# A decoder block: q and k projected with tokens on partitions, turned there, then transposed

## The reference

```
def partial_rotary(t, cos, sin):
    half = ROT_DIM // 2                       # 8
    t1 = t[..., :half]; t2 = t[..., half:ROT_DIM]
    r1 = t1 * cos - t2 * sin
    r2 = t2 * cos + t1 * sin
    return concatenate([r1, r2, t[..., ROT_DIM:]], axis=-1)

h = modulate(rms_norm(x, g_mix), sh1, sc1)
u, q, k, v, ga, gb = split(h @ w_in)
y_ssm = s5_mixer(u, ...)                      # complex diagonal recurrence over the 256 tokens
qh, kh = partial_rotary(heads(q)), partial_rotary(heads(k))
o = causal_attention(qh, kh, heads(v))        # one block of 256 keys
merged = sigmoid(ga) * glu(gelu(y_ssm)) + sigmoid(gb) * (o @ w_attn_o)
x = x + gt1 * (merged @ w_out)
x = x + gt2 * top4_of_32_experts(modulate(rms_norm(x, g_ffn), sh2, sc2))
out = rms_norm(x, g_final)
```

## Time and profile before

| | us |
|---|---|
| median of 3 runs | 1171.04 (1170.08 to 1172.61) |
| profiled execution, whole | 1169.95 |
| its span, first to last instruction | 1168.1 |
| TensorE busy in the span | 1125.0 (96%) |
| VectorE / ScalarE / GpSimd busy | 452.4 / 138.2 / 107.8 |
| DMA, mean over the span | 393 GB/s |

### The profile page before, as it was taken

One profiled execution on the slowest core, in us unless ns is written; L12 is line 12 of the kernel. 1 busy time (PEld: TensorE's weight loads), 2 busy tenths in 40 slices (PEclk: granted clock), 3 DMA queues, 4 the chain that ended last, 5 costly groups with the idle time before them and its releaser, 6 DMA issues.

```text
span 1168.1 us, 17323 instructions
## 1 busy us (share of the span) xinstructions
PE 1125.0 (96%) x7015; PEld 502.1 (43%) x7015; DVE 452.4 (39%) x960; ACT 138.2 (12%) x299; POOL 107.8 (9%) x142
## 2 busy tenths in 40 slices
PE   6999999999999999999999999999999999999996
PEld 5867788654333333333333333333333333333332
DVE  5897767462233222333332223222222222222234
ACT  3213231141000000000000000000000000000002
POOL 2878730000000000000000000000000000000000
PEclk9999999999999999999999999999999999999998
DMA  9993379979999999999999999999999999999995
GB/s 346 320 383 114 108 271 388 418 285 427 422 429 429 430 430 430 431 431 431 435 431 431 431 431 431 430 430 431 430 431 431 431 431 430 431 431 424 429 424 212
DMA packets 49090, 459.53 MB, mean 393 GB/s; under 512 B 8944, under 2 KB 9396, under 8 KB 26784
## 3 DMA queue, kind: packets, MB, share of 16 engines
q1 hardware_dynamic: 48176, 458.19, 94.0%
q10 hardware_dynamic: 880, 0.86, 0.2%
HBM read 457.99 MB, written 1.05 MB: 393 GB/s over the span
## 4 chain that ended last, share of the span: by engine, by line
PE 76%; DMA 19%; DVE 2%; ACT 1%; issue 1%; SPq 1%; DVEq 0%
PE ps L1039 28%; DMA ring<-in_w_gu 16%; PE ps L1081 16%; PE ps L610 8%; PE ps L1014 4%; PE ps L958 3%; PE ps L807 2%; DMA ring<-in_w_down 2%; PE ps L1061 2%; PE ps L825 2%; PE ps L790 1%; PE ps L882 1%; PE ps L607 1%; DMA ring<-in_w_ada 1%; PE ps L1069 1%
## 5 line engine op out<-in xcount | busy, mean ns | idle before, releaser
L1081 PE MATMUL ps<-ring,tmp 128*64 128x512 f32 x1024 | 227.0, 595 | 11.2 <-ACT tmp L1299 9.7
L1039 PE MATMUL ps<-ring,zone 128*64 128x512 f32 x1024 | 227.2, 596 | 10.8 <-DMA ring<-in_w_gu 10.8
L1039 PE MATMUL ps<-zone 128*64 128x512 f32 x1024 | 227.0, 596 | 0.2 <-DVE zone L1731 0.2
L1798 DVE TENSOR_TENSOR x_tok<-x_tok,ps 128x512 f32<-128x512 f32 x128 | 82.0, 682 | 261.1 <-PE ps L1014 258.7
L1081 PEld LDWEIGHTS ps<-ring,tmp 128*64 128x64 f32 x1024 | 83.5, 137 | 134.0 <-issue 130.8
L1039 PEld LDWEIGHTS ps<-ring,zone 128*64 128x64 f32 x1024 | 70.6, 137 | 163.1 <-issue 142.6
L1039 PEld LDWEIGHTS ps<-zone 128*64 128x64 f32 x1024 | 70.6, 137 | 152.8 <-issue 146.2
L1296 ACT ACTIVATE hT<-hT 128x256 f32<-128x256 f32 x64 | 23.9, 417 | 725.0 <-DVE hT L1813 725.0
L610 PE MATMUL ps<-hT,ring 128*128 128x256 f32 x448 | 101.5, 382 | 0.9 <-DVE hT L1463 0.9
L1813 DVE TENSOR_SCALAR hT<-ps 128x256 f32<-128x256 f32 x64 | 24.2, 420 | 191.4 <-PE ps L1039 191.4
L610 PEld LDWEIGHTS ps<-hT,ring 128*128 128x128 f32 x448 | 83.6, 190 | 14.4 <-issue 3.5
(11 more groups left out here) (330 smaller groups left out, 828.1 us busy)
## 6 DMA issues: line engine op xcount, KB each, us to landing
ring<-in_w_down SPq DMA_DIRECT2D x61, 2048.0 KB, 18.6
zone<-in_w_gu SPq DMA_DIRECT2D x23, 4096.0 KB, 27.7
ring<-in_w_gu SPq DMA_DIRECT2D x23, 4096.0 KB, 31.3
zone<-in_w_gu SPq DMA_DIRECT2D x14, 2048.0 KB, 12.9
ring<-in_w_gu SPq DMA_DIRECT2D x13, 2048.0 KB, 13.8
ring<-in_w_ada SPq DMA_DIRECT2D x24, 1024.0 KB, 13.0
ring<-in_w_in SPq DMA_DIRECT2D x16, 1024.0 KB, 14.2
ring<-in_w_gu SPq DMA_DIRECT2D x10, 1024.0 KB, 9.1
```

The costliest lines, as they stand in the source:

```text
L1039: last = mm(ps[CAP * h:CAP * h + CAP, b, :], hg[:, 2 * j + kk, :], w[:, kk, D * b + 512 * h:D * b + 512 * h + 512], start=False, stop=(j = ...
L1081: last = mm(ps[CAP * h:CAP * h + CAP, 3, :], actT[:, q, j, :], w[:, q, 512 * h:512 * h + 512], start=False, stop=(j == DN_PIECES - 1 and q ...
L1798: V.tensor_tensor(x_tok[:, t, 512 * h:512 * h + 512], x_tok[:, t, 512 * h:512 * h + 512], ps[:, bank + h, :], ALU.add).then_inc(S["comb_ad ...
```

## The change

q and k are projected in v's form, tokens on partitions, into `q_tok` and `k_tok`, which are other views of the buffers `qT` and `kT`. VectorE turns the first 16 dimensions of each head there with four instructions per tensor, in place. TensorE then transposes the tile in eight 128x128 pieces into two PSUM banks, and ScalarE copies these back over the same buffer, now with channels on partitions. The cosine and sine tables shrink to 32 columns each and the permutation goes, so the constants in HBM have 600 columns in place of 1432. `rotary(0)` moves into the middle of VectorE's last doubling, ahead of the nop for which GpSimd waits; `rotary(1)` stays between the first two recurrences. The second tensor's TensorE part (`turned_columns(1)`) comes after two of the four blocks of `proj(3, 0)`, where the permutation came after one.

```
--- before.py
+++ after.py
@@ -49,8 +49,9 @@
 
 
 C_ID, C_TRI, C_SLOT, C_TRI32, C_ID32, C_Q, C_E, C_MB, C_MC, C_SL = 0, 128, 256, 320, 352, 384, 400, 401, 403, 405
-C_COS, C_SIN, C_ROT, C_CAUSAL = 408, 664, 920, 1048
-C_ALL = 1432
+C_COS, C_SIN, C_CAUSAL = 408, 440, 472
+C_ALL = 600
+C_BIAS = 408
 BF16 = mybir.dt.bfloat16
 
 R_C, R_GMIX, R_D, R_ADA, R_WIDE, R_GFFN, R_ALL = 0, 8, 16, 20, 36, 68, 76
@@ -66,19 +67,12 @@
     p = np.arange(P)
     c[:, C_ID:C_ID + P] = np.eye(P)
     inv = (1.0 / THETA ** (np.arange(0, 2 * HALF, 2, dtype=np.float32) / (2 * HALF))).astype(np.float32)
-    ang = np.arange(T, dtype=np.float32)[None, :] * inv[p % HALF][:, None]
-    turned = (p % HD < 2 * HALF)[:, None]
-    c[:, C_COS:C_COS + T] = np.where(turned, np.cos(ang), 1.0)
-    c[:, C_SIN:C_SIN + T] = np.where(turned, np.sin(ang), 0.0)
-    for j in range(P):
-        if j % HD < HALF:
-            c[j + HALF, C_ROT + j] = -1.0
-        elif j % HD < 2 * HALF:
-            c[j - HALF, C_ROT + j] = 1.0
+    ang = (np.arange(TT, dtype=np.float32)[None, :, None] * P + p.astype(np.float32)[:, None, None]) * inv[np.arange(2 * HALF) % HALF]
+    c[:, C_COS:C_COS + 2 * HALF * TT] = np.cos(ang).reshape(P, -1)
+    c[:, C_SIN:C_SIN + 2 * HALF * TT] = (np.sin(ang) * np.repeat([-1.0, 1.0], HALF)).reshape(P, -1)
     c[:, C_TRI:C_TRI + P] = p[:, None] < p[None, :]
     past = np.where(p[None, :] <= p[:, None], 0.0, -1e30)
     c[:, C_CAUSAL:C_CAUSAL + P] = past
-    c[:, C_CAUSAL + 2 * P:C_CAUSAL + 3 * P] = past
     c[:, C_SLOT:C_SLOT + CAP] = np.arange(1, CAP + 1)
     e = np.arange(EXPERTS)
     c[:EXPERTS, C_TRI32:C_TRI32 + EXPERTS] = e[:, None] <= e[None, :]
@@ -107,7 +101,7 @@
     x_tok = sb("x_tok", [P, TT, D])
     xn_tok = sb("xn_tok", [P, TT, D])
     hT = sb("hT", [P, KD, T])
-    cst = sb("cst", [P, C_ALL])
+    cst = sb("cst", [P, C_BIAS + D])
     ones = sb("ones", [P, P])
     cols = sb("cols", [P, R_ALL])
     mod = sb("mod", [P, 6 * KD])
@@ -131,6 +125,7 @@
     esin = cut(ST * T).rearrange("p (s t) -> p s t", s=ST)
     qT = cut(KW * T).rearrange("p (m t) -> p m t", m=KW)
     kT = cut(KW * T).rearrange("p (m t) -> p m t", m=KW)
+    q_tok, k_tok = (a.rearrange("p m t -> p (m t)").rearrange("p (i n) -> p i n", i=TT) for a in (qT, kT))
     oT = cut(KW * T).rearrange("p (m t) -> p m t", m=KW)
     v_tok = cut(TT * W).rearrange("p (i n) -> p i n", i=TT)
     BT = cut(2 * KW * P).rearrange("p (r m n) -> p r m n", r=2, m=KW)
@@ -217,7 +212,7 @@
     wr2 = ptmp[:, 256:512].rearrange("p (k e) -> p k e", k=KD)
     gfin_row = [xn_tok[32 * h:32 * h + 1, 0, 0:W] for h in range(2)]
     poswt, pickwT = xn_tok[:, 1, 0:2 * T], xn_tok[:, 1, 2 * T:3 * T]
-    brow = cst[:, C_COS:C_COS + D]
+    brow = cst[:, C_BIAS:C_BIAS + D]
     rowT = brow[3 * EXPERTS:P, 0:2 * T].rearrange("p (j t) -> p j t", j=2)
     wr = probs[:, 0:256].rearrange("p (k e) -> p k e", k=KD)
     rt = probs[:, 256:640].rearrange("p (j i e) -> p j i e", j=6, i=TT)
@@ -245,7 +240,7 @@
     more_rows_in, more_cols_up, shift_set = sem("more_rows_in"), sem("more_cols_up"), sem("shift_set")
     names = """x_in const_in rows_in ssm_in late_in gfin_in out_stored ones_set cols_up cols_sb cond_set ssm_rows sprm_up sprm_sb Bblk_set Cblk0_set
         Cblk1_set BT_up CT0_up CT1_up BT_sb CT0_sb CT1_sb phases modrow_sb modT_up mod1_sb sq1 xn1 xT_up
-        hD_sb hA_sb proj_sb bu_up scanned xs_set xs_read rot_up rot_read rope_set sc_up negmax expd probs
+        hD_sb hA_sb proj_sb bu_up scanned xs_set xs_read rotated turned_up turned_sb sc_up negmax expd probs
         probsT_up probsT_sb o_up o_sb mod2_sb row_up row_sb y_skip gelu sig_ga sig_gb sigb_set ya_set
         yb_used merged out_up x1 sq2 xn2 x2T_up h2_sb logit_up top_set ex_set sel_set pos_up pos_sb pos_half rT_up
         rT_sb extra_set cum_up hot_set item_up item_sb hotb_set pick_set hg_up hg_sb gated sig_set
@@ -337,7 +332,7 @@
         return wo[:, 2 * n:2 * n + 2, :]
 
     PROJ_BANK = (0, 2, 0, 2, 0, 0, 0, 4)
-    ROT_BANK = (2, 0)
+    TURN_BANK = (2, 0)
     MOD_BANK = {1: 6, 2: 2}
     LAST_BANK = (6, 0)
     GU_PIECES, DN_PIECES = 4, 2
@@ -421,7 +416,7 @@
 
             for n in range(place["in", 3] + 1):
                 load_piece(n)
-            sp.dma_start(cst[:, P:], const[:, P:]).then_inc(S["const_in"], 16)
+            sp.dma_start(cst[:, P:C_ALL], const[:, P:]).then_inc(S["const_in"], 16)
             for r, (b, cc) in enumerate(((b_re, c_re), (b_im, c_im))):
                 sp.dma_start(b_in[:, r], b[0].rearrange("(s q) p c -> (q p) s c", q=2)).then_inc(S["const_in"], 16)
                 sp.dma_start(c_in[:, r], cc[0].rearrange("(m g) c p -> (g c) m p", m=KW)).then_inc(S["const_in"], 16)
@@ -591,9 +586,9 @@
                     elif g < 4:
                         pe.wait_ge(S["proj_sb"], g - 1)
                         if g == 3:
-                            pe.wait_ge(S["rot_read"], 1)
+                            pe.wait_ge(S["turned_sb"], 1)
                     elif g == 4:
-                        pe.wait_ge(S["rot_read"], 2)
+                        pe.wait_ge(S["turned_sb"], 2)
                     elif g < 7:
                         pe.wait_ge(S["proj_sb"], g)
                     else:
@@ -602,8 +597,8 @@
                     k = 4 * h + kk
                     if g == 0:
                         pe.wait_ge(S["hA_sb" if k % 4 > 1 else "hD_sb"], 2 * h + k % 2 + 1)
-                    if g == 3:
-                        for i in range(TT):
+                    if 1 <= g <= 3:
+                        for i in range(ms[0] // 2, ms[-1] // 2 + 1):
                             last = mm(ps[:, b + i, :], hT[:, k, P * i:P * i + P], w[:, kk, :], start=(k == 0), stop=(k == KD - 1))
                     else:
                         for m in ms:
@@ -662,22 +657,22 @@
                                                Cblk[:, r, m].rearrange("p q n -> p (q n)"), ident)
                 last.then_inc(S[f"CT{r}_up"], 1)
 
-            def rotate(src, n):
+            def turned_columns(n):
 
                 pe.wait_ge(S["proj_sb"], 2 + n)
-                pe.wait_ge(S["const_in"], 80)
+                pe.wait_ge(S["rotated"], n + 1)
                 for m in range(KW):
-                    last = mm(ps[:, ROT_BANK[n] + m // 2, (m % 2) * T:(m % 2) * T + T], cst[:, C_ROT:C_ROT + P], src[:, m, :],
-                              start=True, stop=True, skip_group_check=True)
-                last.then_inc(S["rot_up"], 1)
-
+                    for i in range(TT):
+                        c0 = (m % 2) * T + P * i
+                        last = nc.tensor.transpose(ps[:, TURN_BANK[n] + m // 2, c0:c0 + P], (q_tok, k_tok)[n][:, i, P * m:P * m + P], ident)
+                last.then_inc(S["turned_up"], 1)
 
             HEAD_BANK = (2, 3)
 
             def scores(p):
 
                 if p == 0:
-                    pe.wait_ge(S["rope_set"], 2)
+                    pe.wait_ge(S["turned_sb"], 2)
                     pe.wait_ge(S["proj_sb"], 4)
                     pe.wait_ge(S["mask_set"], 2)
                 else:
@@ -725,15 +720,15 @@
             proj(1, 1)
             proj(2, 0)
             b_columns()
-            rotate(qT, 0)
+            turned_columns(0)
             c_columns(0)
             c_columns(1)
             proj(2, 1, (0,))
             b_u(0)
             proj(2, 1, (1, 2, 3))
-            proj(3, 0, (0,))
-            rotate(kT, 1)
-            proj(3, 0, (1, 2, 3))
+            proj(3, 0, (0, 1))
+            turned_columns(1)
+            proj(3, 0, (2, 3))
             b_u(1)
             proj(3, 1)
             for p in range(HEADS // 2):
@@ -1171,6 +1166,12 @@
                 act.wait_ge(w_used, done["in", 2 * g + 1])
                 nc.scalar.copy(dst, ps[:, b:b + 2, :].rearrange("p b (m t) -> p (b m) t", t=dst.shape[2])).then_inc(S["proj_sb"], 1)
 
+            def turned(n):
+
+                act.wait_ge(S["turned_up"], n + 1)
+                b = TURN_BANK[n]
+                nc.scalar.copy((qT, kT)[n], ps[:, b:b + 2, :].rearrange("p b (m t) -> p (b m) t", t=T)).then_inc(S["turned_sb"], 1)
+
             def head_pair(p):
                 act.wait_ge(S["negmax"], p + 1)
                 for h in range(2):
@@ -1201,14 +1202,16 @@
                 for q in range(2):
                     nc.scalar.activation(Bblk[:, r, :, q, :], b_sum(r), ACT.Copy,
                                          scale=cst[:, C_MB + q:C_MB + q + 1]).then_inc(S["Bblk_set"], 1)
-            projected(1, qT)
+            projected(1, q_tok)
             act.wait_ge(S["BT_up"], 1)
             nc.scalar.copy(BT[:, :, :, :].rearrange("p r m n -> p (r m n)"), ps[:, 6:8, :].rearrange("p b n -> p (b n)")).then_inc(S["BT_sb"], 1)
             for r in range(2):
                 act.wait_ge(S[f"CT{r}_up"], 1)
                 nc.scalar.activation(CT[:, r].rearrange("p m n -> p (m n)"), ps[:, 4 + 2 * r, :], ACT.Copy,
                                      scale=(1.0 if r == 0 else -1.0)).then_inc(S[f"CT{r}_sb"], 1)
```

(47 more changed lines are left out.)

107 lines of the change are left out of this document (52 added, 55 removed).

## The result

The changed kernel took 1172.6 us, the median of 13 executions (1170.27 to 1174.6), against 1170.08 for the kernel before in 13 executions. (The forecast started from 1171.04, the median of the first three of these.) The ratio is 1.0019, 95% interval 1.0012 to 1.0027. That is within the 0.2% taken as the bound, and inside the forecast range, but its interval excludes 1: the kernel is slower by about 2.2 us, where the sum had said +0.2. The profiled execution took 1172.6 us with a span of 1170.8, 2.7 us more than the span before.

The account below looks back on a forecast made before the run. TensorE's mixer chain sets when the DMA-bound expert weight stream starts running without a gap, and so the end. Terms -1.72 + 1.95 = +0.2 us gave 1171.2 us on the 1171.04 median; range 1168.9 to 1173.4.

Parts of the forecast that it names:

- the term for k: At k's transposes, TensorE waits 1.95 us because `rotary(1)`, disturbed by GpSimd's last doubling, takes 4.2 us.
- One for one: What TensorE gains or loses in the mixer stage reaches the kernel's end in full, as the stream's last gaps move too.
- What goes: On TensorE, transposes replacing both permutations save 1.72 us; the changed form of q and k projections counts nothing.
- q: `rotary(0)` in VectorE's last doubling takes 1.5 us, ending at 62.7, hidden before TensorE asks at 63.8.
- `b_u(1)` within 0.5 us of 83.2: Sign that the forecast is right: TensorE's `b_u(1)` comes within 0.5 us of 83.2.
- rival 1: At k's turn, no lock worth naming: TensorE gains 1.72 us, 0.6 lost at `c_x(0)`; 1169.9 us; chance 0.2.
- GpSimd: Its last doubling starts 1.55 us later, saves 2.5 and pays 0.9: net about 0, slack 1.1 us at `c_x(0)`.
- Rival 2: GpSimd's tables come 2.45 us late, delaying TensorE through `c_x(0)` by 1.35 us; 1172.4 on the median; chance 0.15.
- Elsewhere ... I count nothing: ScalarE's two added copies, 1.0 us each, fall in idle time; constants 1.0 us of DMA shorter; no effect counted.
- Rival 3: TensorE's clock falls to 1.2 GHz around the transposes and stop, 10 us more per 10 us of matmuls; 1181; chance 0.02.

Follow-up runs that it names:

- `late_turn_bias`: Changed kernel with k's transposes after all of `proj(3, 0)` and ScalarE's b_down load issued after its sigmoids: 1168.98 us, ratio 0.9987 to before.
- the control: The changed kernel run again, unaltered, beside the kernel before: 1173.15 us, ratio 1.0020.
- `psum_k`: Changed kernel with `rotary(1)` taking k from PSUM, so no instruction has both inputs in SBUF: 1170.12 us, ratio 0.9998 to before.
- `wide_const`: Changed kernel with its constants padded to the old 1432 columns: 1172.59 us, ratio 1.0016 to before.
- `late_turn_negate`: Changed kernel with k's transposes after all of `proj(3, 0)` and row maxima negated by ScalarE, not VectorE: 1168.74 us, ratio 0.9989 to before.
- `before_negate`: Kernel before with only the row maxima negated by ScalarE in place of VectorE: 1170.5 us, ratio 0.9999.
- `all_three`: Changed kernel with k's transposes after all of `proj(3, 0)`, 64 idle TensorE instructions and ScalarE negating row maxima: 1168.55 us, ratio 0.9983 to before.

## Why the prediction was right, and where it was not

**The time.** Forecast 1171.2 and within 0.2%; measured 1172.6 and within 0.2%. But the forecast was +0.2 us on the kernel before, and the measured difference is +2.2 by the ratio. In the profiled stretch it is +1.60, 1.4 more than the sum: 0.6 of it lies in the term for k, and most of the rest in a step that I counted at nothing. That the range still held 1172.6 is in part luck: it reached +2.4 us from a median of before that was 1 us above the one of 13 executions, and the medians now differ by 2.5.

**One for one: right.** In all fourteen profiles 73.66 to 73.69 us lie between the modulation's first sum and the experts, and in twelve of them 910.98 to 911.95 from there to the end, without a trend over starts of the experts from 254.76 to 260.65. In two (the second profile of before, and `late_turn_bias`) it was 912.8: scatter of the expert stage itself.

**What goes: right.** Undisturbed groups of eight transposes took 0.87 and 0.88 us where the permutations took 1.73. The changed form of the projections cost nothing: 32 instructions of it took 13.73 us on the chain, 0.429 each.

**q: right.** Turned at 63.70, asked for at 64.6, no wait; each instruction at its undisturbed length.

**k: right in mechanism, small in size.** Four instructions of "0.7, then 1.1 and twice 1.2" were 0.80, 1.09, 1.43 and 1.15, and began at 75.79 where I had 74.85. That is only the later start of 1.0; from the start of the stretch it is 32.79 against a forecast of 32.86. The four durations with the gaps between them made 4.57 and not 4.2 us (I had said "with the gaps", but 0.7, 1.1 and twice 1.2 are 4.2 without them), and the wait was 2.36 (2.11 in the control) against 1.95. Its restart added 0.19: the eight transposes behind it took 1.06 on the chain and not 0.87. The term of 1.95 measured 2.55. So the sign "`b_u(1)` within 0.5 us of 83.2" failed: it began at 84.93, and counted from the start of the stretch 0.80 later than before.

The Trainium skill (SBUF — State Buffer, "Who interferes with whom") has the rule that decided between my case and rival 1: a VectorE instruction with two SBUF inputs and a GpSimd instruction that reads SBUF exclude each other for the whole instruction. Here both sides were measured, 4.57 us with two SBUF inputs and 1.54 with one in PSUM. The same section says that a VectorE instruction of the tensor_scalar kind can contend in the same way; the row of 1.28 us at 94.82 beside 0.17 at 96.63 agrees, and I had not applied it.

**GpSimd: right in the outcome, not in its terms.** There was no wait at `c_x(0)`. From the start of the stretch GpSimd's last doubling began 1.50 us later than before (I had 1.55), and its twelve instructions took 13.5 us together and not 15.5: the old `rotary` had cost them 2.1 (in `psum_k` they took 13.4), not 2.5, and the new one costs 0.1, not 0.9. So GpSimd was early, and idled 1.36 us for VectorE's scans before its second set of results. These came 57.62 us after the start of the stretch (before, 57.54); the slack grew from 1.1 to 1.8 us because TensorE came later. Rival 2 did not happen, yet its path is real: when GpSimd was made to yield, 1.34 us came out at that very place.

**"Elsewhere ... I count nothing": wrong, and this is the step that failed.** It asked what the change adds to each queue of work and to the DMA, and not what moves when TensorE's program gets shorter. Half a packet less of code put a fetch on ScalarE's late loads, which lengthened one issue by 0.9 us and set back the modulation's sum by 0.96 (1.06). The sum as measured: -1.72 + 2.36 + 0.19 = +0.83 at `b_u(1)`, where the rows read 41.93 - 41.13 = +0.80 from the start of the stretch. Between `c_x(0)` and `b_u(3)` before lost 0.13 that after did not. Then +0.93 up to the modulation's sum: +1.60. In the control, -1.72 + 2.11 + 0.19, 0.52 more at `b_u(3)` than before and 1.06 at the sum make +2.16. The second of these, a wait of up to 0.65 us by the phase between VectorE and GpSimd, was missed too.

**Rival 1** (no lock, 1169.9) is what `psum_k` built: 1170.12. The two times are near only because the kernel before took 1170.42 beside it, and not 1171.04: against before the rival had -1.1 us, and d was -0.26. No 0.6 us were lost at `c_x(0)`, while 1.57 were at the two places that I had not seen. **Rival 3** (the clock) happened once, in `wide_const`, and cost 1.7 us and not 10: I had priced 10 us of matmuls at the low level, and it was over within a few.

**Open.** The medians differ by 2.5 us (2.7 in the control's group), and by the ratios by 2.2 to 2.3; the two profiles account for 1.6 and 2.2. Late rises and falls of the clock in some executions could hold the rest, but only profiled executions show where they lie. The mean granted clock, which every execution has, points that way: 0.9970 over the 13 executions after and over the 11 of the control, 0.9977 over the 33 of before beside the control. As an estimate, 0.0007 of 1170 us is 0.8 us of full-speed time. Why TensorE's fetch goes with a longer issue on ScalarE is not shown either. Shown is that they coincide in all eight profiles that have the slow issue, of seven kernels (`late_turn_negate` is the eighth: packet at 168.3, issue ended at 169.7), and in none of the other six (`before_negate` has its packets at 158.2 and 185.9, `all_three` at 161.9 and 187.7), and that moving the fetch by idle instructions frees the issue, in two kernels.
